# Bias tables of a sparse attention, worked out in an earlier feed-forward and kept in DRAM

## What is computed

```python
def rel_bucket(dist):
    max_exact = REL_BUCKETS // 2
    n = jnp.maximum(dist, 0)
    nf = jnp.maximum(n.astype(jnp.float32), 1.0)
    log_b = max_exact + (jnp.log(nf / max_exact) / math.log(REL_MAX_DIST / max_exact)
                         * (REL_BUCKETS - max_exact)).astype(jnp.int32)
    return jnp.where(n < max_exact, n, jnp.minimum(log_b, REL_BUCKETS - 1))
...
bias = rel_table[rel_bucket(posq[:, :, None] - take_rows(positions, sel))]
logits = jnp.einsum('bqhd,bqkd->bqhk', qb, k_sel).astype(jnp.float32) * A_HEAD_DIM ** -0.5
logits = logits + jnp.swapaxes(bias, 2, 3).astype(jnp.float32)
valid = sel <= q_idx[None, :, None]
logits = jnp.where(valid[:, :, None, :], logits, NEG_INF)
p = jax.nn.softmax(logits, axis=-1).astype(v.dtype)
return jnp.einsum('bqhk,bqkd->bqhd', p, v_sel)
```

## Time and profile before

| | us |
|---|---|
| median of 3 runs | 2256.41 |
| lowest, highest | 2253.2, 2266.82 |
| the profiled execution, own time | 2262.77 |
| its span, first to last instruction | 2261.0 |
| TensorE busy | 2153.3 (95%) |
| VectorE busy | 1343.9 (59%) |
| ScalarE busy | 874.1 (39%) |
| mean granted TensorE clock | 0.954 |

### The profile page before, as it was taken

The page is one execution under the profiler, slowest core; times in us unless marked ns, Lnnn a source line. Parts: engine busy times, 40 slices in busy tenths (PEclk is TensorE's granted clock), DMA queues, the critical chain, the costliest instruction groups (busy, mean ns, idle before and its releaser), DMA issues.

```text
span 2261.0 us, 26296 instructions
## 1 busy us (share of the span) xinstructions
PE 2153.3 (95%) x10663; PEld 1695.4 (75%) x10665; DVE 1343.9 (59%) x2279; ACT 874.1 (39%) x1453; POOL 154.2 (7%) x101
## 2 busy tenths in 40 slices
PE   5999999999999998999999998999889999999998
PEld 4755788888877966687888887877555688888886
DVE  7697478847835466547643655368876564633632
ACT  4455544424423255524433433232553433422421
POOL 0463100000010000010000000000000001000000
PEclk9998989999999999889999999999985999999998
DMA  8442226565431210112332321222100022333331
GB/s 299 131 150 84 75 73 210 188 199 177 154 98 56 79 63 29 38 38 88 104 95 92 97 95 59 84 83 62 41 20 2 11 95 83 106 95 98 93 93 65
DMA packets 61753, 214.80 MB, mean 95 GB/s; under 512 B 6849, under 2 KB 7745, under 8 KB 61633
## 3 DMA queue, kind: packets, MB, share of 16 engines
q1 hardware_dynamic: 61632, 213.12, 29.4%
HBM read 211.00 MB, written 2.10 MB: 94 GB/s over the span
## 4 chain that ended last, share of the span: by engine, by line
PE 83%; DVE 11%; ACT 3%; issue 2%; DMA 0%; POOL 0%; SPq 0%; DVEq 0%; POOLq 0%; ACTq 0%
PE bank L286 23%; PE bank L288 22%; PE bank L287 22%; PE bank L291 14%; DVE bank L1083 4%; PE bank L788 2%; DVE wlo L326 1%; DVE steps L841 1%; DVE tmp L520 1%; DVE Hl L525 1%; ACT pr L761 1%; ACT whi L313 1%; DVE sc L1960 0%; DVE steps L1958 0%; DVE pr L753 0%
## 5 line engine op out<-in xcount | busy, mean ns | idle before, releaser
L286 PE MATMUL bank<-Hh,whi 128*128 128x512 f32 x1632 | 651.0, 399 | 32.9 <-DVE wlo L326 8.2
L288 PE MATMUL bank<-Hh,wlo 128*128 128x512 f32 x1632 | 641.6, 393 | 0.0
L287 PE MATMUL bank<-Hl,whi 128*128 128x512 f32 x1632 | 641.1, 393 | 0.0
L326 DVE TENSOR_TENSOR wlo<-stg,whi 128x1024 fp32r<-128x1024 f32 (+1 forms) x299 | 358.8, 1205 | 435.6 <-ACT whi L313 435.0
L313 ACT ACTIVATE whi<-stg 128x1024 fp32r<-128x1024 f32 (+1 forms) x309 | 313.7, 1026 | 443.4 <-PE bank L288 436.0
L286 PEld LDWEIGHTS bank<-Hh,whi 128*128 128x128 f32 x1632 | 310.0, 190 | 106.8 <-issue 8.4
L288 PEld LDWEIGHTS bank<-Hh,wlo 128*128 128x128 f32 x1632 | 309.8, 190 | 66.5
L287 PEld LDWEIGHTS bank<-Hl,whi 128*128 128x128 f32 x1632 | 310.4, 190 | 61.8 <-issue 0.2
L288 PE MATMUL bank<-HIDh,wlo 128*128 128x512 f32 x352 | 140.3, 399 | 0.0
L287 PE MATMUL bank<-HIDl,whi 128*128 128x512 f32 x352 | 138.8, 394 | 0.0
L286 PE MATMUL bank<-HIDh,whi 128*128 128x512 f32 x352 | 138.3, 393 | 0.0
(11 more groups left out here) (288 smaller groups left out, 2819.3 us busy)
## 6 DMA issues: line engine op xcount, KB each, us to landing
raw<-in_mod_w SPq DMA_DIRECT2D x96, 512.0 KB, 4.2
stg<-in_ffn_in SPq DMA_DIRECT2D x88, 512.0 KB, 4.2
stg<-in_ff SPq DMA_DIRECT2D x64, 512.0 KB, 3.5
stg<-in_ffn_out SPq DMA_DIRECT2D x40, 512.0 KB, 3.6
stg<-in_cm_w SPq DMA_DIRECT2D x24, 512.0 KB, 4.2
stg<-in_gates SPq DMA_DIRECT2D x16, 512.0 KB, 3.6
stg<-in_z_ch SPq DMA_DIRECT2D x12, 512.0 KB, 3.5
stg<-in_w_k SPq DMA_DIRECT2D x8, 512.0 KB, 3.6
```

What stands on the lines that cost most here:

```text
L286: pe.e.matmul(out_, l[0], r[0], start=start, stop=False, skip_group_check=True)
L287: pe.e.matmul(out_, l[0], r[1], start=False, stop=False, skip_group_check=True)
L288: return pe.e.matmul(out_, l[1], r[0], start=False, stop=stop, skip_group_check=True)
L326: hand.e.tensor_tensor(wlo[j % NW][:, 0:n * c], stg[j % NSTG][:, 0:n * c], whi[j % NW][:, 0:n * c].bitcast(F32), ALU.subtract).then_inc(*m ...
```

## The change

The tables are made during the down products of the second feed-forward, one step in each turn of `within`, TensorE four turns behind VectorE, into banks 5 and 7. `FIRST`, the step and its 12 matmuls are the same. ScalarE copies each four steps' bank into one of two buffers and stores it itself (256 KB) into a DRAM tensor `bias_kept` of 20 such pieces. What is not done after three groups of the second part's down products (6 steps on TensorE, 2 on VectorE) is done there at once, ahead of the last group. `table_dve` runs with the first step. The casts of positions move to the head of the rotation work; the key positions are loaded there too. In the sparse attention four loads, one per query block, bring the tables back (512 KB, 1, 1.5 and 2 MB), each into a place of its own, at four points of the latent and the sparse attention; the step buffers and `lead_dsa` are gone from it, and it gets a fourth bank for scores (5) and a second for transposes (4). The diff, without the lines that only declare semaphores and buffers:

```diff
-                    dve.e.tensor_tensor_reduce(p[:, 0:N], banks[self.score_bank(i, c)][:, 0:N], it["in1"], -it["scale"], 3e38,
+                    o, s = p[:, 0:N], banks[self.score_bank(i, c)][:, 0:N]
+                    if "cut" in it:
+                        o, s = (x.rearrange("p (u j) -> p u j", j=it["cut"]) for x in (o, s))
+                    dve.e.tensor_tensor_reduce(o, s, it["in1"], -it["scale"], 3e38,
                                                ALU.add, ALU.min, self.col(i, 2 * c)).then_inc(*dve_done.up((self.name, "soft", i, c)))
...
+                    if inside and part == 0:
+                        tables = inside[0]()
+                    pe.within[:] = [tables] if inside else []
                     gemm(*down, 3, lambda m: [(by[0], (by[1], l, m))])
-                    pe.within[:] = [sums_within(sy, 6)] if part else []
+                    if part:
+                        all_of(pe.within[0] if inside else ())
+                        pe.within[:] = [sums_within(sy, 6)]
                     gemm(*down, 1, lambda m: [(by[0], (by[1], l, m))], 6)
                     pe.within[:] = []
                 sum_last(sy)
...
-                    beside_gemm(act, f"ffn_out{l}", a, b, 4, evac_y)
+                    if inside and part == 0:
+                        tables = inside[1]()
+                    act.within[:] = [tables] if inside else []
+                    beside_gemm(act, f"ffn_out{l}", a, b, 3, evac_y)
+                    if part:
+                        all_of(act.within[0] if inside else ())
+                        act.within[:] = []
+                    beside_gemm(act, f"ffn_out{l}", a, b, 1, evac_y, 6)
+                    act.within[:] = []
                 act.beside[:] = []
...
-                    beside_gemm(dve, f"ffn_out{l}", a, b, 4, evac_y)
+                    if inside and part == 0:
+                        tables = inside[2]()
+                    dve.within[:] = [tables] if inside else []
+                    beside_gemm(dve, f"ffn_out{l}", a, b, 3, evac_y)
+                    if part:
+                        all_of(dve.within[0] if inside else ())
+                        dve.within[:] = []
+                    beside_gemm(dve, f"ffn_out{l}", a, b, 1, evac_y, 6)
+                    dve.within[:] = []
...
+            posk, posq = sb("posk", [P, P], I32, ph), sb("posq", [P, S], F32, ph)
+            td, tt_, Tb = sb("td2", [P, H], F32, ph), sb("tt2", [P, 4 * H], F32, ph), sb("Tb2", [P, 3, 4 * H], BF16, ph)
+            step8 = sb("step8", [P, 8, S], BF16, ph)
+            out_b = [sb(f"out_b{i}", [P, S], F32, ph) for i in range(2)]
             ph.close()
+            sc2 = cst[:, C_IQ:C_IQ + P]
+            BIAS_BANKS = [5, SPREAD]
...
             def vector():
                 dve.wait_ge(s_posi, 16)
                 dve.wait_ge(s_cst, 16)
                 dve.e.tensor_copy(a1[R2, :], posi[R2, :]).then_inc(*dve_done.up())
+                dve.e.tensor_copy(posq[:, :], posi[:, :]).then_inc(*dve_done.up("posq"))
+                dve.wait_ge(s_posk, 16)
+                dve.e.tensor_copy(sc2, posk[:, :]).then_inc(*dve_done.up())
                 dve.wait_ge(*dve_done.now)
+                dve.e.tensor_scalar(sc2, sc2, cst[:, C_THR:C_THR + 1], None, ALU.add).then_inc(*dve_done.up("sc2"))
...
+                sp.e.dma_start(posk[:, :], ins["pos_k"]).then_inc(s_posk, 16)
                 yield
...
+            STEPS = 4 * FIRST[4]
+            def bias_pe():
+                for u in range(-4, STEPS):
+                    if u >= 0:
+                        b = BIAS_BANKS[u // 4 % 2]
+                        if u % 4 == 0:
+                            open_bank(b, [(act_done, ("ds", "bias", u // 4))])
+                        pe.wait_ge(*dve_done["ds", "step", u])
+                        for x in range(4):
+                            g = 4 * (u % 4) + x
+                            for y in range(3):
+                                tok = mm(banks[b][:, 32 * g:32 * g + 32], step8[:, u % 8, x * P:(x + 1) * P], Tb[:, y, :], y == 0, y == 2)
+                        tok.then_inc(*core_done.up(("ds", "step", u)))
+                    yield
+            def bias_act():
+                for m in range(-2, FIRST[4]):
+                    if m < 0:
+                        for _ in range(4):
+                            yield
+                        continue
+                    act.wait_ge(*core_done["ds", "step", 4 * m + 3])
+                    if m > 1:
+                        act.wait_ge(s_bias[m % 2], 16 * (m // 2))
+                    act.e.activation(out_b[m % 2].rearrange("p (h j) -> p h j", h=H),
+                                     banks[BIAS_BANKS[m % 2]][:, :].rearrange("p (j h) -> p h j", h=H), ACT.Copy).then_inc(
+                        *act_done.up(("ds", "bias", m)))
+                    act.wait_ge(*act_done["ds", "bias", m])
+                    act.e.dma_start(bias_kept[m], out_b[m % 2][:, :]).then_inc(s_bias[m % 2], 16)
+                    for _ in range(4):
+                        yield
+            def bias_dve():
+                table_dve("ds", 16, td, tt_, Tb)
+                for qb in range(4):
+                    for u in range(4 * FIRST[qb], 4 * FIRST[qb + 1]):
+                        c = 4 * (u - 4 * FIRST[qb])
+                        if u >= 8:
+                            dve.wait_ge(*core_done["ds", "step", u - 8])
+                        dve.wait_ge(*dve_done["sc2"])
+                        dve.wait_ge(*dve_done["posq"])
+                        dve.e.tensor_tensor(step8[:, u % 8, :].rearrange("p (x q) -> p x q", x=4),
+                                            posq[:, qb * P:(qb + 1) * P].unsqueeze(1).to_broadcast([P, 4, P]),
+                                            sc2[:, c:c + 4].unsqueeze(2).to_broadcast([P, 4, P]), ALU.is_ge).then_inc(
+                            *dve_done.up(("ds", "step", u)))
+                        yield
+            return (vector, scalar, sync), (bias_pe, bias_act, bias_dve)
+        rotation, bias_inside = rotation_parts()
+        ffn_stage(1, *rotation, ("wo1", DT - 1), "z", vcol("attn_norm_g_2", 0, 8), bias_inside)
...
-            B2 = [sb(f"B2{i}", [P, H, S], F32, pa) for i in range(2)]
+            B2 = [sb(f"B2{qb}", [P, 2 * qb + 2, H, 64], F32, pa) for qb in (3, 2, 1)][::-1]
             stat_a = sb("stat_a", [P, 8 * 4 * 3], F32, pa)
+            pa.close()
+            B2.insert(0, sb("B20", [P, 2, H, 64], F32, pa))
...
                 b = OB["dsa"][n % 2]
-                return {"N": N, "in1": B2[qb % 2][:, h, 0:N], "in1_ready": lambda: [act_done["ds", "bias", FIRST[qb + 1] - 1]],
+                return {"N": N, "in1": B2[qb][:, :, h, :], "in1_ready": lambda: [(s_b2[qb], 16)], "cut": 64,
                         "scale": 0.125, "mask": (identb[:, :], Msel[:, QOFF[qb]:QOFF[qb] + N]),
...
-            dsa = Core("dsa", [dsa_item(h, qb) for qb in range(4) for h in range(H)], [0, 1, 2], [3], sq, SC + [ROT], stat_a, 1)
+            dsa = Core("dsa", [dsa_item(h, qb) for qb in range(4) for h in range(H)], [0, 1, 2, 5], [3, 4], sq, SC + [ROT], stat_a, 1)
...
-                all_of(dsa.tensor(None, lead_dsa(lambda qb: steps_pe("ds", 4 * FIRST[qb], 4 * (FIRST[qb + 1] - FIRST[qb]), Tb, [4, 5]))))
+                all_of(dsa.tensor())
...
-                dve.wait_ge(s_posq, 16)
-                dve.e.tensor_copy(posq[:, :], tmp[0][:, :].bitcast(I32)).then_inc(*dve_done.up("posq"))
-                dve.wait_ge(s_posk, 16)
-                dve.e.tensor_copy(sc2, tmp[1][:, 0:P].bitcast(I32)).then_inc(*dve_done.up())
-                dve.wait_ge(*dve_done.now)
-                dve.e.tensor_scalar(sc2, sc2, cst[:, C_THR:C_THR + 1], None, ALU.add).then_inc(*dve_done.up("sc2"))
-                table_dve("ds", 16, td, tt_, Tb)
...
-                all_of(dsa.vector(dsa_close_dve, lead_dsa(biases)))
+                all_of(dsa.vector(dsa_close_dve))
...
+                for i in range(2):
+                    act.wait_ge(s_bias[i], 160)
...
-                sp.wait_ge(*dve_done["x", "z", 4])
-                sp.e.dma_start(tmp[0][:, :].bitcast(I32), ins["pos_q"]).then_inc(s_posq, 16)
-                sp.wait_ge(*dve_done["x", "z", 5])
-                sp.e.dma_start(tmp[1][:, 0:P].bitcast(I32), ins["pos_k"]).then_inc(s_posk, 16)
+                def bias_in(qb):
+                    sp.e.dma_start(B2[qb].rearrange("p u h j -> p u (h j)"),
+                                   bias_kept[FIRST[qb]:FIRST[qb + 1]].rearrange("u p c -> p u c")).then_inc(s_b2[qb], 16)
                 beside_first(sp, "z_ch")
                 beside_gemm(sp, "z_ch", 0, DT, 4)
                 beside_gemm(sp, "gates", 0, DT, 8)
                 next_block(sp, "w_uv", 0)
+                for i in range(2):
+                    sp.wait_ge(s_bias[i], 160)
                 for j in range(4):
                     heads_sp(j)
+                sp.wait_ge(*core_done["mla", "S", 23, 0])
+                bias_in(0)
```

(6 more changed lines are left out.)

42 lines of the change are left out of this document (8 added, 34 removed).

## The result

The changed kernel takes 2277.22 us (median of ten, 2264.31 to 2285.11) against 2262.66 for the kernel before (median of ten, 2252.97 to 2267.71): ratio 1.0062, 95% interval 1.0045 to 1.0079. The forecast was 2239.0 with a range of 2226 to 2254, built on the 2256.41 of the three executions shown ahead of it; by its ratio of 0.9922 it would be 2245 on 2262.66. The sign is wrong and the range missed.

A forecast was written before the change was run, and what follows sets the result against it. The prediction took TensorE's own stream to bound the kernel (83% of the chain of waits). Its terms, -52.8 - 1.9 + 37.0 = -17.7 us, gave ratio 0.9922 and 2239 us on the median, range 2226 to 2254.

The forecast's parts named there:

- Part 1: Sparse attention without its tables: 56.6 us saved if the clock holds, 52.8 us with some items at half clock.
- five items at half clock, 3.8 us: Start of the sparse attention: clock falls at the gap, five small items run slow, costing 3.8 us of the saving.
- far end: Upper bound on the sparse attention's clock loss: all of the first two query blocks at half clock, 11.6 us.
- half clock through the first two query blocks: Rival, sparse attention: clock loss 11.6 us instead of 3.8, total change -9.9 us, 2246.5 us; chance 0.20.
- Part 2: Table products inside the second feed-forward's down products, with stall and moved casts: 37.0 us added, bounds 28 and 52.
- the six steps issued together: Remaining table steps ahead of the last group of down products, the last two waiting for VectorE: 2.6 us.
- The single step: One table step between wide down products, change-over included: 0.385 us, 74 of them 28.5 us.
- The stall: Early in the down products TensorE waits for VectorE's step 0: 3.0 us, plus 1.9 us for the clock falling.
- Part 3: Start of the last block: without casts and table on VectorE, TensorE starts earlier, 1.9 us saved.
- Part 4: The four loads bringing tables back into the sparse attention: hidden behind earlier items, no cost.
- the clock stays at half level in the down products: Rival, from the stall on: 0.2 us more per wide matmul, +40 us in total, 2296 us; chance 0.05.
- The clock holds everywhere: Rival: no clock fall after the stall or in the sparse attention, -23.4 us in total, 2233 us; chance 0.22.

The follow-up runs named there:

- e1: Changed kernel plus eight unused wide products (128x512) filling TensorE's gap ahead of the sparse attention's first transpose; 2248.19 us, ratio 0.9928 to the kernel before.
- e3: Changed kernel plus twelve unused wide products in one go ahead of the transposes of the sparse attention's ninth item; 2249.43 us, ratio 0.9943.
- e5: Changed kernel plus nine narrow score products, not wide ones, filling the gap ahead of the sparse attention's first transpose; 2244.40 us, ratio 0.9925.
- e12: Changed kernel with e1's filled gap, steps issued four at a time, and thirty wide products in the idle time starting the latent attention; 2227.99 us.
- e9: Changed kernel plus only three narrow score products ahead of the sparse attention's first transpose, leaving 0.56 us idle; 2275.69 us, ratio 1.0073.
- e10: Changed kernel plus four wide products in the sparse attention's ninth item; of ten executions four took 2250.3 to 2254.2 us, five 2280.0 to 2286.5, one 2261.2.
- e2: Changed kernel plus one wide product ahead of the transposes in each of the sparse attention's first 24 items; 2276.82 us, ratio 1.0058.

## Why the prediction was wrong, point by point

**The step that failed** is in Part 1: "Where nothing of 32 columns lies between, the clock came back soon after TensorE had got busy again", from which it took "five items at half clock, 3.8 us", with the first two query blocks, 11.6 us, as the far end. The clock fell where the forecast had it fall, and did not come back for 65 us, of which TensorE was idle 0.47. It came back in the query block of 512 keys. The evidence was one row of one execution, 0.72 in 1602 to 1605, from the end of a fall and not from its length. That the level came back there among narrow products, 6.2 us behind the restart, is true; but behind the same restart it took up to 14.5 us in other executions, and in the sparse attention the same kind of products went without it for 65. What makes the two stages differ stays open. The far end was cut at two query blocks without a reason. With the level held, e1's stage took 69.0 us, and the forecast's sum without the surcharge was 64.7 + 1.0 + 0.6 behind a start of 3.5, thus 69.8: the item prices were right, and the level alone was wrong. The rival "half clock through the first two query blocks" had the mechanism and less than half of its price (11.6 of 96.3 - 69.8 = 26.5 us).

**The Trainium skill's rule** (page "TensorE: Matmul & The Clock Gate", section "What's actually happening": half clock is the default, activity releases it) spoke against the change at this very place, and I gave it 0.20. e3 agrees with it, since the level came back during twelve wide products; the changed kernel does not, since TensorE was busy 63.53 of 64 us and stayed at half level. That pauses between bursts of matmuls let the clock drop is told on the same page of the Trainium skill, section "HAM oscillation — how this bites in real kernels". The pauses told of there are waits for DMA that are longer than some 2 us of matmuls; here 1.02 us of idle time was enough, as e1 and e5 against the changed kernel show.

**Part 2** was right in its mechanism and 2.8 us short: 38.8 measured against 36.0. The mis-sized term is the six steps issued together, 5.2 us instead of 2.6: the forecast gave the waits there no fall of the clock (1.6 us) and had VectorE's last step at its usual 0.68. The single step was nearly right, 0.40 instead of 0.385, or 74 x 0.015 = 1.1 us. The stall was forecast at 3.0 and measured at 2.50, with 1.3 for the clock instead of 1.9.

**Part 3** (1.9 forecast, 2.0 measured) and **Part 4** (no item waits for a load) were right. So were the casts, forecast at 1.0: VectorE begins the split behind them 0.96 us later (1032.04 against 1031.08), and TensorE's wait for it is 1.6 us instead of 0.4. That the whole stretch up to the down products is 0.9 longer proves nothing, since it differs by ten us between executions.

**Not in the forecast at all** were 4.8 us of clock in the latent attention, and 2.8 at the end. Both differ between executions of the same code by as much, so the change did not cause them; a forecast by stages has to allow for them. Why the same restart leaves half level at times after 6 and at times after 14 us isn't settled; in e12, where the gap ahead of it is filled, it doesn't fall to it.

**The rivals.** That the clock stays at half level in the down products (0.05) did not happen: 1.00 from 1163 to 1405. "The clock holds everywhere" (2233) is, in the attention, what e1 made of the change with 2 us of useless work; its 2248 is on 2262, the forecast's 2233 on 2256.

## What to carry to other kernels

A gap on TensorE is to be priced by the stage behind it, not by its length: one microsecond idle at the head of the sparse attention cost 27 us, because its narrow products went on at the level that they had. So look at the head of each stage that has no wide matmuls, fill its gap with harmless products until the waits show none, and only then judge what a change to the stage is worth. Where short products are put between wide ones, issue several steps' products together: 0.07 of the 0.40 us a step came back that way, and most of the waits with it. And a time to recover that is read from one execution is one sample: measure it in several before a forecast rests on it.

## What the runs showed of the hardware that I had not expected

- TensorE at 0.50 while busy 63.53 of 64 us (changed kernel), 65 of 65 (e9) and 80 of 80 (e10), with the items' own products (in e10 and four wide ones); and 1.00 over 70 us of the same products (e5).
- It is no law of narrow products: in the latent attention of the kernel before the level came back at 1603.7 among scores of 96x128, and behind the same restart it was back after 6.2 to 7.5 us in eight traces and after 12.7 to 14.5 in five.
- Idle time alone does not tell whether the clock falls: 0.56 us (e9) and 0.59 us (e2) were followed by half level; 0.75 and 0.77 us behind thirty wide products (e12) and 0.57 us at 1708.68, among the narrow products of the latent attention (changed kernel), were not. A gap of 1.96 us ahead of 1691.30 was followed by half level from 1691.9 to 1695.3 in the changed kernel, the same gap in e1 (1.95 us, ahead of 1688.69) by none. What decides between them stays open.
- Twelve wide products brought the level back in the trace of e3, and by the times (2247.8 to 2253.9 us) in all its four executions; four of them did so in four or five of ten (e10): the same program ends 30 us apart.
- One wide product an item, 24 of them, did nothing for the level (e2).
